# Starting the matmul operands at multiples of 256 bytes in a two-block transformer kernel

## The reference, cut to what matters

```python
def reference(x, c, ctx, ..., norm_final_g_2):
    x = first_block(...)     # two layers: adaptive norm, w_in, three kinds of attention, w_out
    return second_block(x, ...)

def second_block(x, meta_tokens, ...):
    h = jnp.concatenate([meta, x], axis=1)                  # 16 + 256 tokens, 2048 channels
    hn = rms_norm(h, norm_mix_g)
    u, gb_in, gc_in, v_in, ga_lin, gbr_lin = jnp.split(hn @ w_in, splits, axis=-1)
    y_a = jnp.einsum("blgc,gcd->blgd", causal_multiscale_pool(u), pool_w) * pool_scale
    y_b = (gb_in * causal_depthwise_conv(gc_in * v_in, conv_w)) @ conv_out_w
    g_a, g_b = jnp.split(sigmoid(concat([ga_lin, gbr_lin]) + b_gate), 2, axis=-1)
    h = h + (g_a * y_a + g_b * y_b) @ w_o
    gate, up = jnp.split(rms_norm(h, norm_ffn_g) @ w_gate_up, 2, axis=-1)
    h = h + (jax.nn.silu(gate) * up) @ w_down
    return rms_norm(h, norm_final_g)[:, N_META:]
```

## Time and profile before

| | |
|---|---|
| median of 3 runs | 3424.82 us (3418.18 to 3427.82) |
| the profiled execution | 3425.93 us, its span 3424.6 us |
| busy in the span | PE 3291.0 us (96%), PEld 2854.7 (83%), DVE 1654.1 (48%), ACT 1359.8 (40%), POOL 172.1 (5%) |
| moved by DMA | 566.09 MB, mean 165 GB/s |

### The profile page before, as it was taken

The page is one execution under the profiler, slowest core; times in us unless marked ns, Lnnn a source line. Parts: engine busy times, 40 slices in busy tenths (PEclk is TensorE's granted clock), DMA queues, the critical chain, the costliest instruction groups (busy, mean ns, idle before and its releaser), DMA issues.

```text
span 3424.6 us, 52152 instructions
## 1 busy us (share of the span) xinstructions
PE 3291.0 (96%) x21958; PEld 2854.7 (83%) x21958; DVE 1654.1 (48%) x2688; ACT 1359.8 (40%) x2179; POOL 172.1 (5%) x252
## 2 busy tenths in 40 slices
PE   6899999978999999999899999999999999999998
PEld 2588888863458879887459999999999999999998
DVE  1322233374663354344585675565555645445444
ACT  2322233343443254334454443344444444444343
POOL 2001000011001101000201000000000000000000
PEclk9899999998999989999899999999999999999999
DMA  8633222226644246433425455555555455555554
GB/s 304 244 119 127 94 93 92 85 68 237 256 177 148 99 176 202 145 128 113 155 84 197 156 184 185 185 182 188 186 188 187 166 187 189 185 187 189 185 186 153
DMA packets 152826, 566.09 MB, mean 165 GB/s; under 512 B 17520, under 2 KB 17648, under 8 KB 151440
## 3 DMA queue, kind: packets, MB, share of 16 engines
q1 hardware_dynamic: 146160, 529.52, 44.4%
q0 software_dynamic: 6432, 33.23, 2.7%
HBM read 550.10 MB, written 12.58 MB: 164 GB/s over the span
## 4 chain that ended last, share of the span: by engine, by line
PE 90%; DMA 4%; DVE 3%; ACT 1%; POOL 1%; issue 1%; SPq 0%; POOLq 0%; DVEq 0%; ACTq 0%
PE ps L743 20%; PE ps L745 20%; PE ps L744 20%; PE ps L732 7%; PE ps L734 7%; PE ps L733 7%; DMA sb_raw<-in_stream 3%; PE ps L653 2%; PE ps L865 1%; PE ps L851 1%; PE ps L828 1%; PE ps L844 1%; PE ps L819 1%; PE ps L660 1%; DMA sb_rope<-in_rope 1%
## 5 line engine op out<-in xcount | busy, mean ns | idle before, releaser
L1287 DVE TENSOR_TENSOR sb_wlo<-sb_raw,sb_whi 128x1024 fp32r<-128x1024 f32 (+1 forms) x814 | 992.4, 1220 | 1313.6 <-ACT sb_whi L937 1312.5
L937 ACT ACTIVATE sb_whi<-sb_raw 128x1024 fp32r<-128x1024 f32 (+1 forms) x818 | 859.4, 1051 | 1132.3 <-PE ps L745 887.2
L743 PE MATMUL ps<-sb_hn_hi,sb_whi 128*128 128x256 f32 (+4 forms) x2944 | 830.3, 282 | 4.1 <-DVE sb_hn_lo L1359 4.1
L744 PE MATMUL ps<-sb_hn_lo,sb_whi 128*128 128x256 f32 (+4 forms) x2944 | 829.4, 282 | 0.0
L745 PE MATMUL ps<-sb_hn_hi,sb_wlo 128*128 128x256 f32 (+4 forms) x2944 | 828.4, 281 | 0.0
L743 PEld LDWEIGHTS ps<-sb_hn_hi,sb_whi 128*128 128x128 f32 x2944 | 556.3, 189 | 5.2 <-DVE sb_hn_lo L1359 4.5
L745 PEld LDWEIGHTS ps<-sb_hn_hi,sb_wlo 128*128 128x128 f32 x2944 | 556.8, 189 | 0.0
L744 PEld LDWEIGHTS ps<-sb_hn_lo,sb_whi 128*128 128x128 f32 x2944 | 556.3, 189 | 0.0
L734 PE MATMUL ps<-sb_whi,sb_lo 128*128 128x512 f32 (+1 forms) x968 | 374.3, 387 | 0.0
L732 PE MATMUL ps<-sb_whi,sb_hi 128*128 128x512 f32 x896 | 354.2, 395 | 0.0
L743 PE MATMUL ps<-sb_hi,sb_whi 128*128 128x512 f32 (+1 forms) x1024 | 348.8, 341 | 3.4 <-DVE sb_wlo L1287 3.4
(11 more groups left out here) (265 smaller groups left out, 4035.5 us busy)
## 6 DMA issues: line engine op xcount, KB each, us to landing
sb_raw<-in_stream SPq DMA_DIRECT2D x992, 512.0 KB, 3.3
sb_raw<-in_stream SPq DMA_DIRECT2D x18, 384.0 KB, 2.9
sb_T<-in_x POOLq DMA_DIRECT2D x1, 4096.0 KB, 17.5
z_scratch<-sb_scr POOLq DMA_DIRECT2D x16, 256.0 KB, 2.5
sb_zb<-z_scratch POOLq DMA_DIRECT2D x16, 256.0 KB, 3.2
sb_bias<-in_bias POOLq DMA_DIRECT2D x4, 1024.0 KB, 10.0
x_scratch<-sb_T POOLq DMA_DIRECT2D x1, 4096.0 KB, 15.3
sb_T<-in_x POOLq DMA_DIRECT2D x2, 1536.0 KB, 7.5
```

Source lines behind the costliest of these rows:

```text
L743: PE.matmul(o, whi[:, s, w], xh, start=k == 0, stop=False)
L744: PE.matmul(o, whi[:, s, w], xl, start=False, stop=False)
L937: AC.activation(whi[:, s, 0:width], raw[:, r, 0:width], ACT.Copy).then_inc(*hi.up((g.id, c)))
L1287: VE.tensor_tensor(wlo[:, s, 0:width], raw[:, r, 0:width], whi[:, s, 0:width].bitcast(F32), ALU.subtract).then_inc(*lo.up((g.id, c)))
```

## The change

Three things change, all of them addresses. `place` is rounded up to 256 ahead of `raw`, which moves `raw`, `whi`, `wlo` and `block` up by 192 bytes, so that they begin at multiples of 256. The tiles of block two that hold 256 tokens get rows of 256 floats (1024 bytes). `hn_hi` and `hn_lo` get rows of `NS` = 320 floats (1280 bytes), and their tokens are put at the end of a row, so that the last 256 begin at column 64, 256 bytes into the row. RES and the temporaries keep 272.

```diff
+NS = L + HD
...
     rope = own("rope", [P, 4, 2, 2 * HD])
+    place[0] = (place[0] + 255) // 256 * 256
     raw = own("raw", [P, RAW, CH])
...
-    NB = DT * N2 * 4
-    PH = sb("pooled_hi", [P, DT, N2], F32R, block)
-    PL = sb("pooled_lo", [P, DT, N2], F32R, block + NB)
+    LB = DT * L * 4
+    PH = sb("pooled_hi", [P, DT, L], F32R, block)
+    PL = sb("pooled_lo", [P, DT, L], F32R, block + LB)
...
-    FH = sb("ffn_hi", [P, FT, N2], F32R, block)
-    FL = sb("ffn_lo", [P, FT, N2], F32R, block + FT * N2 * 4)
-    hn_at = block + 2 * FT * N2 * 4
-    NH = sb("hn_hi", [P, DT, N2], F32R, hn_at)
-    NL = sb("hn_lo", [P, DT, N2], F32R, hn_at + NB)
-    t3_at = hn_at + 2 * NB
-    res_at = block + 153600 - NB
+    FH = sb("ffn_hi", [P, FT, L], F32R, block)
+    FL = sb("ffn_lo", [P, FT, L], F32R, block + FT * L * 4)
+    hn_at = block + 2 * FT * L * 4
+    NH = sb("hn_hi", [P, DT, NS], F32R, hn_at)
+    NL = sb("hn_lo", [P, DT, NS], F32R, hn_at + DT * NS * 4)
+    t3_at = hn_at + 2 * DT * NS * 4
+    res_at = block + 153600 - DT * N2 * 4
...
         if g.x in ("hn", "latent"):
-            a = 0 if g.kind == "ffn" else N2 - g.n
-            return NH[:, k, a:a + g.n], NL[:, k, a:a + g.n]
+            return NH[:, k, NS - g.n:], NL[:, k, NS - g.n:]
...
-            AC.activation(NH[:, k, 0:n], T2[:, 4 + k % 2, 0:n], ACT.Copy).then_inc(*a_ev.up((tag, k)))
+            AC.activation(NH[:, k, NS - n:], T2[:, 4 + k % 2, 0:n], ACT.Copy).then_inc(*a_ev.up((tag, k)))
```

More of the change, by code:

```diff
@@ L473, in build @@
     ZB = sb("zb", [P, 2, 512], F32, s_at + 10 * TB)
-    NB = DT * N2 * 4
-    PH = sb("pooled_hi", [P, DT, N2], F32R, block)
-    PL = sb("pooled_lo", [P, DT, N2], F32R, block + NB)
[L478 to L481, removed]
-    FH = sb("ffn_hi", [P, FT, N2], F32R, block)
-    FL = sb("ffn_lo", [P, FT, N2], F32R, block + FT * N2 * 4)
-    hn_at = block + 2 * FT * N2 * 4
-    NH = sb("hn_hi", [P, DT, N2], F32R, hn_at)
-    NL = sb("hn_lo", [P, DT, N2], F32R, hn_at + NB)
-    t3_at = hn_at + 2 * NB
-    res_at = block + 153600 - NB
-    assert t3_at + 4 * N2 * 4 <= res_at and block + 5 * NB + 4 * (N2 + 2) * 4 <= hn_at
+    LB = DT * L * 4
+    PH = sb("pooled_hi", [P, DT, L], F32R, block)
+    PL = sb("pooled_lo", [P, DT, L], F32R, block + LB)
+    CHI = sb("conv_hi", [P, DT, L], F32R, block + 2 * LB)
+    CLO = sb("conv_lo", [P, DT, L], F32R, block + 3 * LB)
+    YA = sb("ya", [P, DT, L], F32, block + 4 * LB)
+    G4 = sb("g4", [P, 4, L], F32, block + 5 * LB)
+    FH = sb("ffn_hi", [P, FT, L], F32R, block)
[5 more added lines that the diff above has]
+    res_at = block + 153600 - DT * N2 * 4
+    assert t3_at + 4 * N2 * 4 <= res_at and block + 5 * LB + 4 * (N2 + 2) * 4 <= hn_at
     RES = sb("res", [P, DT, N2], F32, res_at)
-    T2 = sb("tmp2", [P, 8, N2 + 16], F32, block + 3 * NB)
+    T2 = sb("tmp2", [P, 8, N2 + 16], F32, block + 3 * LB)
     T3 = sb("tmp3", [P, 4, N2], F32, t3_at)
@@ L494, in build @@
     SCALED = sb("scaled", [P, DT, L], F32, hn_at + 4 * N2 * 4)
-    CV = sb("cv", [P, 4, N2 + 2], F32, block + 5 * NB)
+    CV = sb("cv", [P, 4, N2 + 2], F32, block + 5 * LB)
     PS = nc.alloc_psum_tensor("ps", [P, 8, 512], F32)
@@ L1358, in make_hn @@
             VE.wait_ge(*a_ev.at(tag, k))
-            VE.tensor_tensor(NL[:, k, 0:n], T2[:, 4 + k % 2, 0:n], NH[:, k, 0:n].bitcast(F32),
+            VE.tensor_tensor(NL[:, k, NS - n:], T2[:, 4 + k % 2, 0:n], NH[:, k, NS - n:].bitcast(F32),
                              ALU.subtract).then_inc(*v_ev.up((tag, k)))
```

## The result

The change made the kernel slower: 3442.38 us, median of 6 runs (3434.82 to 3453.46), against 3423.47 for the kernel before on the same chip (6 runs, 3416.11 to 3427.82). The ratio is 1.0056, with a 95% interval of 1.004 to 1.0071. The forecast was 3344 us; the rival that ended on the other side, the clash of operands, gave 3452, which is 10 too much.

What follows compares the result with a forecast made beforehand. PE, busy 96% of the span, was taken as the bound, through the pace of successive matmuls. Gains 42.5 + 10.3 + 30.7 + 2.2 less 5 gave 80.7 us: 3424.8 to 3344 us, 8-in-10 range 3305 to 3372.

Steps and rivals of the forecast that it cites:

- the clash of operands: Rival (5%): moving and stationary operands beginning at the same place within 256 bytes cost time; 256-column matmuls 120 ns, 3452 us.
- What those 10 ns hang on: Extra time per matmul: a moving start at 0 saves 6.7 ns against 64, about 5 against 128 or 192.
- the first rival: Rival (13%): the 6.7 ns left at 0 come from the stationary start; up to 72 us more gain, 3272 us.
- The second trial: Layer 1's output product, rows of `hi` at 64 for every `k`: 25 starts in 3.00 us, even 120 ns.
- Item 1: Block two's 10,368 matmuls of 256 columns: from 117.4 to 113.3 ns each, 42.5 us gained.
- Item 2: The 1,536 matmuls of 256 columns on `hi`: from 120 to 113.3 ns each, 10.3 us gained.
- Item 3: 4,576 matmuls of 512 columns gain 6.7 ns each, 30.7 us; the 384-column ones of `wqb` 2.2 us.
- The second rival: Rival (12%): long matmuls of 512 columns gain nothing, 3377 us, or half, 3360 us.
- Item 4: The mixer's 258-column groups and other `u` groups: zero gain, bounds 3.5 us either way.
- Item 5: Stationary operands going from 64 to 0: taken as zero, with up to 72 us gain at the other end.
- Item 6: Gain not reaching the end: ada pieces waiting for weights and longer DVE waits before transposes, together 5 us lost.
- A mix of starts: Sign of error: the pace at 0 belongs to the mix, `k` = 3 coming behind three slow ones; no size given.

Runs made afterwards that it cites:

- the last kernel: Changed kernel with block two's tiles 192 bytes up, plus layer 1's output-product tokens written 192 bytes further: 3378.38 us, 0.9866 of the kernel before.

## Why the prediction was wrong

**What failed is the reading under "What those 10 ns hang on".** It took the fast `k` = 3 as one "whose moving rows begin at 0". The same rows say as much of a distance of 192 from the stationary, whose start the first rival knew to be "64 in every row of the trace that is float32r", and the clash of operands named it. What seemed to speak against the clash, that "128 and 192 share nothing with 64 and still cost 118.3", excludes only that a shared place is the one cost, not that places count relative to each other. The second trial, `hi` at 64 with an even 120 ns, was d = 0 and had the answer: 120 ns is what all these matmuls would take after the change. The chance of 5% was far too small for a reading that fitted the rows as well.

- *Item 1*, -42.5 us: +25.1, with the sign turned. 117.7 went to 120.0 ns, not to 113.3. The size of the gain at a good place was right: block two's matmuls took 42.0 us less than before in the last kernel, 38.7 with block two alone at 192 and 32.3 with the weights at 64, by how many stretches fell on the fast pace.
- *Item 2*, -10.3 us: 0, since d was 0 before and after. 10.3 was right as the worth of d = 192: all 1,536 gave 9.7 us with the weights at 64, the 768 of the output product 4.8 in the last kernel.
- *Item 3*, -33 us: 0, for the same reason, and it would have failed with every layout tried. It rested on the extra being "a constant per matmul", 13.3 ns for 256 and 512 columns alike at d = 0. The equality holds, but for 512 columns no place that was tried takes a part of it away: they take 226.7 ns at d = 0, 228.9 at 64 and 233.3 at 192. The second rival, which doubted the long matmuls, had the right doubt for the wrong cause.
- *Item 4*: held as no term. In the timeline below of the changed kernel, two starts of 258 columns are 24 matmuls apart: 2.87 us, 119.6 ns, beside 119.2 from the earlier trace rows; over the trace the 2,304 matmuls of this item took 1.6 us less.

```profile
2046.80 0.28 PE L744 MATMUL ps<-sb_hn_hi,sb_whi 128*128 128x258 f32 x1
...
2049.67 0.28 PE L744 MATMUL ps<-sb_hn_hi,sb_whi 128*128 128x258 f32 x1
```

- *Item 5*: the stationary does matter, through d. Its own start does not: the rounding alone moved it from 64 to 0 at a ratio of 0.9989.
- *Item 6*: the stream's waits grew by 3.4 us, DVE's by 0. The feed, DVE's and ACT's cover held, up to 194 GB/s.
- *The clash*: right in direction, place and size of the term (120.0 ns everywhere, 836 matmuls for 834, 25.1 us for 27). That the span grew by 27.6 is in part luck, since the profiled execution was the slowest of six; the medians moved by 18.9. A shared place is the one that is slow in every stretch, as this rival had it. But it is not alone in costing: d = 128 gave 118.3 (in whole pieces), 64 and 192 gave 117.8 or 113.3.
- *A mix of starts*, the last sentence of the prediction: not the cause of `k` = 3, since an even stream of d = 192 can be as fast. But how a stretch began, or what stands between its matmuls, does count at d = 64 and 192.
- The Trainium skill, "SBUF — State Buffer", Door 1, puts a penalty on crossing to a new line of 16 bytes; by it alone, starts that are all multiples of 16 would give one pace. The runs differ by 6.7 ns between d = 0 and 192, so it does not tell the paces apart here.

What stays open is the mechanism. It is shown that the pace of float32r matmuls with a load before each depends on the places of the moving and the stationary operand relative to each other, on the number of columns, and on what ran before: the pieces at other distances, or the head of the stretch. Which read meets which load, what picks one of the two paces, and why 512 columns prefer what 256 avoid, is not. The Trainium skill, "TensorE: Matmul & The Clock Gate", Part 2, gives TensorE two independent read ports of SBUF, one for the moving operand and one for loads, so that a load takes no read bandwidth from a running matmul; that the pace changes when only one side is shifted (836 to 885 matmuls in 100 us) doesn't fit two reads that leave each other alone, but no run here shows where they meet.

## What to carry to other kernels

When a trace offers a natural trial, list what stood still in it: here one operand never moved, so an absolute place and a distance could not be told apart, and one shift of a single side (64 bytes ahead of the weights, one line) would have told them. Try such a relative shift before laying buffers out anew; here it was worth 1.0%, and 1.3% where only 256-column operands were moved, while matmuls of 512 columns were best left at a distance of 0. Round both operands to the same boundary only if the runs say so: with equal starts, both at 0 or both at 64, 256 columns took 120 ns in every stretch.

And look at more than one window, in more than one trace: a pace that is constant over 100 us can still be one of two, and the same kernel can draw the other in its next stretch.

## What the runs showed of the hardware

- Moving all operands together by 192 bytes changed nothing (853 matmuls in 100 us against 852); moving one side against the other by 64 changed the pace of 256-column matmuls by up to 6.7 ns (836 to 885 in 100 us).
- 256 columns: 120.0 ns at d = 0 in 30 stretches of 30; at d = 192, 113.3 ns in 26 of 37 and 117.8 in the others; at d = 64, 113.3 in 6 of 30 and 117.8 in the others. A stretch without interruption kept its pace, up to 6,300 matmuls.
- 512 columns: 226.7 ns at d = 0, 228.9 at 64, 233.3 at 192.
- One and the same pair of places (moving 0, stationary 192) gave 113.3 ns for a piece of 24 matmuls between pieces at other distances, and 117.8 in the feed-forward of an even kernel.
